# A decoder step whose first layer opens with the input instead of the memory prompt

## What is computed

```python
mem_n   = rmsnorm(mem_prompt[None], mem_norm[:, None, None, :])
mem_k_p = einsum('lbmd,ldk->lbmk', mem_n, w_mem_k)   # both layers, width 256
mem_v_p = einsum('lbmd,ldk->lbmk', mem_n, w_mem_v)

z = rmsnorm(h, w['a_norm1'][a]) @ w['a_w_in'][a]
q = rope(z[..., :RET_W] ...)                   # 6 heads of 128
k = rope(z[..., RET_W:2 * RET_W] ...) * RET_HD ** -0.5
v, g = z[..., 2 * RET_W:3 * RET_W], z[..., 3 * RET_W:4 * RET_W]
qm = z[..., 4 * RET_W:]                        # memory queries, width 256
s_new, o = retention(ret_s0[a], q, k, v)
mix = head_groupnorm(o) * silu(g)
om = mem_attend(qm, mem_k[l], mem_v[l])        # prompt rows: mem_k_p; sample rows: cached
h = h + concatenate([mix, om]) @ w_out
```

## Time and profile before

| | us |
|---|---|
| median of three runs | 1627.74 (1625.76 to 1630.88) |
| profiled execution, its own time | 1629.53 |
| span of its trace | 1627.7 |
| PE busy | 1537.8 (94%) |
| DVE busy | 821.3 (50%) |
| ACT busy | 570.1 (35%) |

### The profile page before, as it was taken

The page is one execution under the profiler, slowest core; times in us unless marked ns, Lnnn a source line. Parts: engine busy times, 40 slices in busy tenths (PEclk is TensorE's granted clock), DMA queues, the critical chain, the costliest instruction groups (busy, mean ns, idle before and its releaser), DMA issues.

```text
span 1627.7 us, 28935 instructions
## 1 busy us (share of the span) xinstructions
PE 1537.8 (94%) x11449; PEld 1425.3 (88%) x11449; DVE 821.3 (50%) x1290; ACT 570.1 (35%) x889; POOL 50.4 (3%) x76
## 2 busy tenths in 40 slices
PE   3899999979999999999988889999899999999998
PEld 2888888869999999999988556766899999999998
DVE  4847777655433434334575556665454334343344
ACT  4532333323322313223443246554343223131243
POOL 1120000020000000000001000000000000000000
PEclk8999999979999999999999989999999999999999
DMA  6543222333232322323233404542122223232221
GB/s 195 167 137 93 80 79 80 89 102 88 79 91 79 91 79 77 90 77 90 78 82 104 121 16 117 148 123 76 57 74 85 86 79 90 78 90 84 82 79 59
DMA packets 229384, 149.35 MB, mean 92 GB/s; under 512 B 11121, under 2 KB 222466, under 8 KB 229282
## 3 DMA queue, kind: packets, MB, share of 16 engines
q1 hardware_dynamic: 218802, 122.57, 26.2%
q0 software_dynamic: 6032, 20.28, 4.2%
q10 hardware_dynamic: 4448, 5.11, 1.0%
HBM read 140.26 MB, written 7.68 MB: 91 GB/s over the span
## 4 chain that ended last, share of the span: by engine, by line
PE 84%; DVE 9%; ACT 4%; issue 2%; DMA 1%; ACTq 0%; DVEq 0%; SPq 0%
PE ps L597 65%; PE ps L1118 3%; PE ps L1076 3%; DVE wl L1623 2%; PE ps L1145 2%; PE ps L1059 1%; PE ps L1022 1%; PE ps L1023 1%; DVE onorm L1796 1%; PE ps L979 1%; DVE rstd L1642 1%; DVE ml L1627 1%; PE ps L982 1%; ACT wh L1228 1%; DVE gn L1790 1%
## 5 line engine op out<-in xcount | busy, mean ns | idle before, releaser
L597 PE MATMUL ps<-mh,wh 128*128 128x288 f32 (+1 forms) x1424 | 326.2, 298 | 21.3 <-DVE wl L1623 16.9
L597 PE MATMUL ps<-xh,wh 128*128 128x288 f32 x1542 | 336.6, 300 | 8.9 <-DVE wl L1623 7.9
L597 PE MATMUL ps<-xh,wl 128*128 128x288 f32 x1542 | 330.0, 296 | 0.0
L597 PE MATMUL ps<-xl,wh 128*128 128x288 f32 x1542 | 329.9, 296 | 0.0
L597 PE MATMUL ps<-ml,wh 128*128 128x288 f32 (+1 forms) x1424 | 323.5, 296 | 0.0
L597 PE MATMUL ps<-mh,wl 128*128 128x288 f32 (+1 forms) x1424 | 323.5, 296 | 0.0
L1228 ACT ACTIVATE wh<-raw 128x1024 fp32r<-128x1024 f32 (+1 forms) x195 | 202.2, 1037 | 285.4 <-PE ps L597 263.5
L1623 DVE TENSOR_TENSOR wl<-raw,wh 128x1024 fp32r<-128x1024 f32 (+1 forms) x195 | 232.9, 1195 | 74.3 <-ACT wh L1228 72.9
L597 PEld LDWEIGHTS ps<-xh,wh 128*128 128x128 f32 x1542 | 247.9, 190 | 20.1 <-issue 10.1
L597 PEld LDWEIGHTS ps<-mh,wh 128*128 128x128 f32 x1424 | 237.9, 191 | 25.4 <-DVE wl L1623 17.7
L597 PEld LDWEIGHTS ps<-xh,wl 128*128 128x128 f32 x1542 | 249.0, 190 | 0.0
(11 more groups left out here) (299 smaller groups left out, 1310.1 us busy)
## 6 DMA issues: line engine op xcount, KB each, us to landing
raw<-in_w_up SPq DMA_DIRECT2D x64, 512.0 KB, 4.0
raw<-in_w_down SPq DMA_DIRECT2D x64, 512.0 KB, 3.6
pages<-in_cache_mla SPq DMA_DIRECT2D x128, 160.0 KB, 2.2
raw<-in_a_w_in SPq DMA_DIRECT2D x26, 512.0 KB, 3.8
memkc<-in_cache_mem_k POOLq DMA_DIRECT2D x16, 256.0 KB, 4.4
memvc<-in_cache_mem_v POOLq DMA_DIRECT2D x16, 256.0 KB, 5.5
raw<-in_a_w_out SPq DMA_DIRECT2D x8, 512.0 KB, 3.6
raw<-in_b_w_out SPq DMA_DIRECT2D x8, 512.0 KB, 3.7
```

What stands on the lines that cost most here:

```text
L597: last = mm(ps[:, 2 * (m % 2) + c, 0:n], w[:, s, kk, :], x(kk, col, n), start=(kk == 0 and nth == 0), stop=(kk == final and nth == 2))
```

## The change

Steps 1 to 6 of the opening are reordered and some are done in another way; the loop over heads, and all that follows, is the same but for its first turn and for counts of semaphores.

- **Order of the products**: two query tiles, four tiles of head 0, then the eight memory tiles (before: memory, query, head 0). The query tiles are numbered 0 and 1 (`M_Q`), head 0 is 2 to 5 (`M_Z0`), memory 6 to 13 (`M_MEM`).
- **Query tiles step by step**: `query_step(j, kk)` runs six matmuls, one K tile of query tile j. Between the steps stand the transposes of later K tiles (`x_turn`), each of which needs a pair of banks out of 2 to 7 (`X_BANK`) whose former K tile has been split (`X_AFTER`).
- **Split of the input straight from PSUM**: ACT's `x_head` and DVE's `x_tail` read the transposed K tile in PSUM; the copy to `res` is shared, ACT takes tiles 0, 2, 4 and 6, DVE 1, 3, 5 and 7.
- **Row sums in row layout**: ACT squares whole rows with a sum (`x_squares`, one instruction per 128 rows), takes the root of one column per 128 rows, DVE inverts it and multiplies it into the identity (`row_diagonals`), and PE spreads it with five matmuls against ones (`row_scales`). The same for the memory rows. The chain of L1234, L1633, L1637, L609, L1240 and L1642 goes for the first layer.
- **Loads**: ACT issues, behind the input, the two query weights and the memory rows. SP issues identity, gains, ones, then head 0's four weight tiles, then memory's. POOL issues the rotary tables at once, the cached keys and values when six K tiles are headed, and the masks and decays when the memory is split.
- **Turning memory rows back** (`kv_to_rows`) moves behind memory tiles 5 to 7 and into the first turn of the loop, to banks 4 and 5.

The core of the diff:

```diff
+X_BANK = [4, 6, 2, 4, 6, 4, 6, 4]
+X_AFTER = {3: 0, 4: 1, 5: 3, 6: 4, 7: 5}
@@ SP
-            sp.dma_start(ident[:, :], t["c_ident"]).then_inc(mem_in, 16)
-            for n in range(2):
-                sp.dma_start(memrow[:, n, :], ...).then_inc(mem_in, 16)
+            for dst, name in ((ident, "c_ident"), (gain, "gains"), (ones, "c_ones")):
+                sp.dma_start(dst[:, :], t[name]).then_inc(gain_in, 16)
+            for part in range(4):
+                load(m_z(0, part), wcols(wa, RET_W * part))
@@ POOL
-            pool.wait_ge(xT_ready, 4)
-            for dst, name in ((ropeC, "c_ropeC"), ... (maskS, "c_maskS")):
+            for dst, name in ((ropeC, "c_ropeC"), (ropeS, "c_ropeS")):
+                pool.dma_start(dst[:, :], t[name]).then_inc(consts_in, 16)
-            pool.wait_ge(x_hi, KD)
+            pool.wait_ge(x_hi, KD - 2)
             sample_memory(0)
+            pool.wait_ge(mem_lo, DEPTH * KD)
...
@@ PE
+            def x_turn(kk):
+                b = X_BANK[kk]
+                if kk in X_AFTER:
+                    pe.wait_ge(x_lo, X_AFTER[kk] + 1)
+                for r in range(RT + 1):
+                    if kk == 0:
+                        pe.wait_ge(x_in[r], 16)
...
+            def query_step(j, kk):
+                if j and kk == 0:
+                    pe.wait_ge(x_lo, 3)
+                dense(M_Q + j, tiles(xh), tiles(xl), ready=(x_lo, lambda kk: kk + 1), part=range(kk, kk + 1))
+            def row_scales():
+                pe.wait_ge(diag_ready, 1)
+                pe.wait_ge(gain_in, 16 * 3)
+                pe.wait_ge(x_lo, 7)
+                for r in range(RT):
+                    mm(ps[:, 6, P * r:P * r + P], ones[:, :], t1[:, P * r:P * r + P], ...)
@@ PE, order of the opening
+            x_turn(0..4); query_step(0, 0..2); query_step(1, 0..1); query_step(0, 3)
+            x_turn(5); query_step(1, 2); x_turn(6); query_step(1, 3); query_step(1, 4); query_step(0, 4)
+            x_turn(7); query_step(0, 5); query_step(0, 6); row_scales()
+            query_step(1, 5); query_step(1, 6); query_step(0, 7); memory_turn(0); memory_turn(1)
+            query_step(1, 7); memory_turn(2); memory_turn(3)
+            z_tile(0, 0, scales_between); z_tile(0, 1, keys_between(0)) ... z_tile(0, 3, keys_between(4))
+            sample_turn(0, 0) ... sample_values(0, 0)
+            memory_tile(0); sample_back(0, 0); memory_tile(1); sample_scores(0, 1); memory_tile(2)
+            sample_turn(0, 1); memory_tile(3); sample_values(0, 1); memory_tile(4); sample_back(0, 1)
+            memory_tile(5); kv_to_rows(0); kv_to_rows(1); memory_tile(6); kv_to_rows(2); kv_to_rows(3)
+            memory_tile(7); kv_to_rows(4); kv_to_rows(5)
@@ PE, first turn of the loop
-                            sample_back(0, 1)
+                            kv_to_rows(6)
+                            kv_to_rows(7)
@@ PE, ret_rows
+                pe.wait_ge(kv_rows, 8)
@@ ACT
+            for j in range(2):
+                act.dma_start(raw[:, M_Q + j, :, :], wcols(t["a_w_in"][0], 4 * RET_W + P * j)).then_inc(w_loaded[M_Q + j], 16)
+            for n in range(2):
+                act.dma_start(memrow[:, n, :], ...).then_inc(mem_in, 16)
+            def x_squares(r):
+                act.wait_ge(x_in[r], 16)
+                rows, src = (P, xrow[:, r, :]) if r < RT else (NS, xsrow[:, :])
+                do(f(scratch[0:rows, :], src, ACT.Square, accum_out=vec[0:rows, 48 + r:49 + r]))
@@ DVE
+            def x_tail(kk):
+                if kk % 2 == 0:
+                    dve.wait_ge(res_act, kk // 2 + 1)
+                dve.wait_ge(x_hi, kk + 1)
+                tail(xl[:, kk, :], pair(X_BANK[kk]), G_A1 + kk, xh[:, kk, :], C[x_lo])
```

More of the change, by code:

```diff
@@ L213, in build @@
         ropeS = takeA("ropeS", [P, ROWS])
+        masks = takeA.where[0]
         maskA = takeA("maskA", [P, H_RET, P])
@@ new lines, in x_head, with x_keep, row_roots @@
+            def x_head(kk):
+                act.wait_ge(xT_ready, kk + 1)
+                head(xh[:, kk, :], pair(X_BANK[kk]), G_A1 + kk, C[x_hi])
+            def x_keep(kk):
+                do(f(res[:, kk, :], pair(X_BANK[kk]), ACT.Copy), C[res_act])
+            def row_roots():
+                do(f(vec[0:NS, 48 + RT:49 + RT], vec[0:NS, 48 + RT:49 + RT], ACT.Sqrt, bias=EPS, scale=1.0 / D))
+                do(f(vec[:, 48:48 + RT], vec[:, 48:48 + RT], ACT.Sqrt, bias=EPS, scale=1.0 / D), C[std_ready])
@@ L1823, in z_tile, with gate @@
                     scaled(m, t1[:, :], rstd[:, :])
+            def gate(h):
+                dve.wait_ge(gate_tanh, h + 1)
+                do(stt(z[:, h % 2, 3, :], t2[:, :], 1.0, t1[:, :], ALU.add, ALU.mult))
+            def z_tile(h, part, middle=None, end=None):
+                w_tail(m_z(h, part) + 1)
+                if middle:
+                    middle(h - 1)
+                z_take(h, part)
                 if end:
@@ L1826, in z_tile @@
                 if part == 3:
[L1827 to L1828 removed]
+                    gate(h)
             do(dve.memset(gn[:, :], 1.0))
             do(dve.memset(mem[0]["qblk"][:, :, :, :], 0.0))
[L1832 to L1833 removed]
+            dve.wait_ge(gain_in, 16 * 3)
+            x_tail(0)
+            x_keep(1)
+            x_tail(1)
+            w_tail(M_Q)
+            x_tail(2)
@@ new lines, in _ @@
+            w_tail(M_Q + 1)
+            x_keep(3)
+            x_tail(3)
+            x_tail(4)
+            row_diagonals()
+            x_keep(5)
+            x_tail(5)
+            x_tail(6)
+            x_keep(7)
+            x_tail(7)
+            row_scales()
+            query_tile(0)
+            w_tail(M_Z0)
+            query_tile(1)
+            memory_diagonals()
+            rope_scales()
+            memory_scales()
+            memory_tail(0, 0)
+            memory_tail(0, 1)
+            w_tail(M_Z0 + 1)
```

459 lines of the change are left out of this document (297 added, 162 removed).

## The result

The changed kernel takes 1620.3 us (median of 7, 1619.2 to 1622.3) against 1630.1 of the kernel before on the same chip (median of 7, 1625.8 to 1632.5): 0.9946 of it, 95% interval 0.9934 to 0.9957. That is 9.8 us gained where the forecast was 17.8, and 1620.3 lies above the range of 1604 to 1617. The profiled execution took 1621.3 us, its trace spans 1619.5.

The account below looks back on a forecast made before the run. PE was taken as nearly full from head 1's product on, so only the opening could give: 21.8 + 78.0 + 5.0 = 104.8 us instead of 123.5, less 0.9, is 17.8 gained; 1627.7 - 17.8 gives 1610 us, range 1604 to 1617.

Parts of the forecast that it names:

- The remainder: From head 1's product to the end: same program, about 1504 us as before, within 2 us.
- the five: Rivals: ACT stuck issuing (0.13), split weights pacing memory tiles (0.09), free flow (0.06), gain swallowed (0.04), PE at half clock (0.03).
- Part 1: Opening up to the first query step: ACT done issuing at 9.5 us, first step at 21.8 (bounds 19.7 and 26.8).
- the rival that has ACT stuck: Opening: ACT's queue holds it to 14.4 us, first step at 26.8, 12.8 us gained, 1615 us; chance 0.13.
- Part 2 and 3: First query step to head 1's product: 78.0 us of PE work, 5.0 of waits (least 2, most 9).
- the 3.0 to 3.6 named: Opening's memory tiles: expected spacing in us where nothing stands between them.
- It flows: Opening: ACT free early and waits of 2 us; 1605 us, or 1603 with the half clock hidden; chance 0.06.
- Head 1's product at 104.8 (102 to 108): End of the opening: PE begins head 1's product at 104.8 us instead of 123.5.
- First turn 0.9 later: Loop's first turn: loses `sample_back`, gains two `kv_to_rows`, and `ret_rows` waits for ACT's copies; 0.9 us later in all.
- Half clock for about 4 us, no more: Behind the first query step: granted clock 0.5 for at most about 4 us, costing 1.7 us.
- the rival with PE held at half clock: Query steps, perhaps through head 0: PE stays at 1.2 GHz, slower by over 0.3%, up to 1647 us; chance 0.03.
- A drain of 1.4 us with each table load: ACT's table loads: a skill page adds a 1.38 us drain per switch; the sum used the trace's 1.28 us without it.

Follow-up runs that it names:

- `pad80`: The changed kernel with 80 already met waits in PE's stream behind the turns of the first three input columns; 1609.6 us, 0.9876 of the kernel before.

## Why the prediction was wrong, point by point

- **The remainder.** "I carry the difference from 123.5 unchanged to the end" is the step that failed. The prediction itself named it as its root ("wrong at its root if that remainder grows"): 1504.2 became 1513.5. The sum had no term for the instruction fetch, and put at nothing what the change does to a loop 1,100 us behind it. Four runs show what stands in its place: by its length of 27 instructions the change moved the start of a loop to where each jump back fetches the loop again, for 10.0 us. Without that, the same opening gives 1609.6, against 1610 forecast. That these agree within 0.4 us is luck in part: the trace of `pad80` gains 16.9 us at head 1's product, 0.9 of them go in the first turn, and medians scatter by 2 to 3 us.
- **A missing rival.** None of the five was of this kind. They all asked what the opening or the head loop waits for; the one term that lost the gain is in neither and not an operation at all. The page of before held it: 67 blocks for 67.1 blocks' worth of program, that is, loops that don't refetch.
- **Part 1, ACT free at 9.5, first step at 21.8.** 12.8 and 25.1: 3.3 late, between the forecast and the rival that has ACT stuck (14.4 and 26.8). The mechanism was right, the middle of the bounds was too early. From ACT's freedom to the first step it had 12.3 us, and 12.3 it is (12.8 to 25.1). The input landed a little ahead of what was said.
- **Part 2 and 3, 78.0 of work and 5.0 of waits.** From 25.1 to head 1's product are 80.9 us, and PE is busy for 80.4 of them:

```profile
25.10:106.00 80.90, 80.40 (x644) 76.09 (x644) 55.09 (x94) 46.27 (x79) 14.59 (x23) 1.00 0.53 158
```

  The work was sized 2.4 us under (80.4 with the half clock in it) and the waits 4.5 over; 0.5 is less than even the least named. The last memory tile takes 3.31 us with 0.44 of turns in it (102.71 to 106.02), so two with nothing between them would be 2.9 apart, under the 3.0 to 3.6 named. "It flows" was right on the waits.
- **Head 1's product at 104.8 (102 to 108).** 106.0: right, but with luck, since ACT 3.3 late and the work 2.4 over nearly cancel against the waits 4.5 under. **First turn 0.9 later.** 0.9: right.
- **Half clock for about 4 us, no more.** Right; matmuls came 0.24 us apart from 25.1 to about 29.1 and the rival with PE held at half clock didn't happen.
- **A drain of 1.4 us with each table load.** Here too the next instruction starts 1.30 behind a load of 1.28 (12.79, then 14.09): no drain shows, and the sum that went by the row was right not to have it.

## What to carry to other kernels

When an edit alters the number of instructions in front of a loop on the engine that sets the time, look at the instruction queue's packets before and after: more packets than the program has blocks means that loops are fetched again, and a few met waits where the engine idles anyway may give it back (10.7 us here). Keep an engine's own first work clear of issuing transfers when much is queued: the four extra issues held ACT for 9.4 us and put head 1's product off by 5 to 6 us. And judge small steps by the place where they end in the trace, since clock losses elsewhere move the end by up to 5 us.

## What the runs showed of the hardware

- A jump back to a block that isn't held leaves PE idle for 2.2 to 2.65 us (in layer 1's loop for 2.35 and 1.74). With the 1.2 GHz level and the slower turn behind it a jump costs 5.4 us (10.8 / 2) in layer 2's loop and 6.8 (13.6 / 2) in layer 1's.
- The gap is named after any semaphore that the next instruction also waits for (`wl`, ready 4 us before) or "issue"; neither name leads to the cause.
- A met wait that is an instruction of its own costs PE 0.109 us (27.6 us for 255).
- The same product of 48 matmuls takes 6.24 us in some turns of a loop and 6.40 in others, at the same granted clock; both turns behind a refetch took 6.40.
- Two weight tiles' transfers keep an issuing engine for 1.11 us with nothing ahead of them and for 4.66 behind 2.3 MB.
